# Six transfers of w_down for each expert, three of them between the next expert's first gate and up slices

## The reference, cut to what matters

```python
def expert_choice_ffn(h, w_router, w_gate, w_up, w_down):
    B, S, D = h.shape
    cap = EC_K * S // N_EXPERTS
    aff = jax.nn.softmax((h @ w_router).astype(jnp.float32), axis=-1)
    g, idx = lax.top_k(aff.transpose(0, 2, 1), cap)
    ...
    def run_expert(args):
        wg, wu, wd, ie, ge = args
        xe = h[b_rows, ie]
        he = jax.nn.silu(xe @ wg) * (xe @ wu)
        return (he @ wd) * ge[..., None].astype(h.dtype)
    ye = lax.map(run_expert, (w_gate, w_up, w_down, idx, g))
    return jnp.zeros_like(h).at[b_idx, idx].add(ye)
```

## Time and profile before

| What | Value |
|---|---|
| Median of three runs | 2459.91 us |
| The profiled execution's own time | 2462.03 us |
| Its span, from the first instruction to the last | 2460.2 us |
| TensorE busy | 1929.5 us (78%) |
| VectorE busy | 486.9 us (20%) |
| ScalarE busy | 315.1 us (13%) |
| Mean granted TensorE clock | 0.861 of full speed |
| Read from HBM | 688.96 MB |
| Chain that ended last | TensorE 49%, DMA 33%, SP's queue 8% |

### The profile page before, as it was taken

One profiled execution on the slowest core, in us unless ns is written; L12 is line 12 of the kernel. 1 busy time (PEld: TensorE's weight loads), 2 busy tenths in 40 slices (PEclk: granted clock), 3 DMA queues, 4 the chain that ended last, 5 costly groups with the idle time before them and its releaser, 6 DMA issues.

```text
span 2460.2 us, 28858 instructions
## 1 busy us (share of the span) xinstructions
PE 1929.5 (78%) x11352; PEld 1035.5 (42%) x11352; DVE 486.9 (20%) x1107; ACT 315.1 (13%) x733; POOL 41.2 (2%) x45
## 2 busy tenths in 40 slices
PE   8898999998999998987765666666666656766665
PEld 7774887588568855644211111111112211211111
DVE  3424332126333312152101010001001100110011
ACT  1213111022222100131100000000000000000001
POOL 0010000001010000000000000000000000000000
PEclk9999999999999999998887887787767777787777
DMA  7531543441245333326999999999999999999997
GB/s 257 138 65 39 184 154 120 157 161 64 69 129 180 129 145 128 137 79 275 407 392 422 421 417 419 422 421 418 418 423 421 419 417 424 420 418 418 424 421 315
DMA packets 173982, 694.24 MB, mean 282 GB/s; under 512 B 15452, under 2 KB 65436, under 8 KB 141010
## 3 DMA queue, kind: packets, MB, share of 16 engines
q1 hardware_dynamic: 170930, 683.63, 70.0%
q0 software_dynamic: 2832, 9.45, 1.9%
q10 hardware_dynamic: 144, 0.13, 0.0%
HBM read 688.96 MB, written 4.19 MB: 282 GB/s over the span
## 4 chain that ended last, share of the span: by engine, by line
PE 49%; DMA 33%; SPq 8%; DVE 4%; issue 3%; ACT 1%; DVEq 1%; ACTq 0%; POOL 0%; POOLq 0%
DMA arena<-in_w_up 29%; PE bank L543 20%; PE bank L564 9%; PE bank L954 5%; SPq L393 4%; DMA arena<-in_w_down 4%; SPq L389 3%; PE bank L969 2%; PE bank L550 2%; PE bank L683 1%; DVE arena L1596 1%; PE bank L692 1%; PE bank L753 1%; PE bank L601 1%; PE bank L767 0%
## 5 line engine op out<-in xcount | busy, mean ns | idle before, releaser
L954 PE MATMUL bank<-arena 128*32 128x512 f32 (+1 forms) x3072 | 482.2, 782 | 305.5 <-DMA arena<-in_w_up 264.2
L543 PE MATMUL bank<-arena 128*128 128x256 f32 (+1 forms) x2720 | 499.9, 345 | 6.8 <-ACT arena L991 3.4
L543 PEld LDWEIGHTS bank<-arena 128*128 128x128 f32 x2720 | 443.5, 192 | 62.8 <-issue 4.7
L954 PEld LDWEIGHTS bank<-arena 128*32 128x32 f32 x3072 | 111.6, 139 | 672.8 <-DMA arena<-in_w_up 358.0
L969 PE MATMUL bank<-arena 128*32 128x256 f32 x2816 | 255.3, 480 | 85.6 <-DMA arena<-in_w_down 85.5
L564 PE MATMUL bank<-arena 128*128 128x512 f32 x544 | 235.5, 593 | 1.2 <-ACT arena L1174 1.2
L969 PEld LDWEIGHTS bank<-arena 128*32 128x32 f32 x2816 | 84.5, 126 | 249.3 <-issue 218.3
L1596 DVE TENSOR_TENSOR arena<-arena,bank 64x256 f32<-64x256 f32 x96 | 38.6, 402 | 750.4 <-ACT arena L1193 748.7
L564 PEld LDWEIGHTS bank<-arena 128*128 128x128 f32 x544 | 102.7, 190 | 127.6 <-issue 126.1
L1193 ACT ACTIVATE arena<-bank 64x512 f32<-64x512 f32 (+1 forms) x48 | 23.2, 550 | 835.8 <-PE bank L954 835.8
L1475 DVE SCALAR_TENSOR_TENSOR arena<-bank,arena 128x254 f32<-128x254 f32 (+1 forms) x176 | 76.8, 478 | 194.6 <-ACT arena L1133 191.3
(11 more groups left out here) (259 smaller groups left out, 1205.1 us busy)
## 6 DMA issues: line engine op xcount, KB each, us to landing
arena<-in_w_down SPq DMA_DIRECT2D x364, 512.0 KB, 12.8
arena<-in_w_gate SPq DMA_DIRECT2D x128, 1408.0 KB, 19.4
arena<-in_w_up SPq DMA_DIRECT2D x128, 1408.0 KB, 22.4
arena<-in_w_up SPq DMA_DIRECT2D x44, 1024.0 KB, 7.5
arena<-in_w_in SPq DMA_DIRECT2D x40, 1024.0 KB, 7.4
arena<-in_w_down SPq DMA_DIRECT2D x16, 1024.0 KB, 5.6
arena<-in_w_out SPq DMA_DIRECT2D x12, 1024.0 KB, 7.1
bias_rows<-arena POOLq DMA_DIRECT2D x1, 3072.0 KB, 46.4
```

What stands on the lines that cost most here:

```text
L543: last = mm(ps[bank][:, j * S + lo:j * S + lo + n], w[:, k, c:c + P], xT[:, k, lo:lo + n], start=(k == 0), stop=(k == KT - 1))
L954: last = mm(ps[b][32 * q:32 * q + 32, 0:n], expert_x[:, k, :], gate_up_ring[:, s_, q // 2, c:c + n], start=(k == 0), stop=(k == KT - 1))
```

## The change

In the expert stage w_down is loaded in six pieces in place of 22 blocks. A half of w_down (1408 rows) is cut into pieces of 512, 512 and 384 rows (`PIECES`). In a piece of n rows each of the 128 partitions holds n/128 neighbouring rows of w_down, that is 4, 4 or 3 rows of 4 KB that lie one behind the other in memory. So a transfer is 2048 KB or 1536 KB, with 16 KB or 12 KB for each partition, and the ring is three buffers of 4, 4 and 3 rows, the same 11 rows as before. The multiplication that makes the hidden values (L1596) reads its inputs with a stride, so that the hidden rows come out in the order that the pieces have. TensorE's matmuls are the same in number and shape; it waits once for each piece and frees a buffer once for each piece.

SP's order changes too. For each expert it is now: slices 4 to 7, pieces 0, 1, 2, the next expert's slices 0 and 1, piece 3, the next expert's slice 2, piece 4, its slice 3, piece 5.

The diff, cut to its core:

```diff
-        down_ring = down_region.take(D_RING, D)
+        down_ring = [down_region.take(n // P, D) for _, n in PIECES]
...
-            def down(e, k):
-                sp.dma_start(down_ring[:, k % D_RING, :], a["w_down_2"][0, bass.ds(e, 1), k * P:(k + 1) * P, :].rearrange("o p n -> (o p) n")
-                             ).then_inc(sem(f"d_in{k % D_RING}"), 16)
+            def down(e, j, ahead=0):
+                b = j % len(PIECES)
+                c0, n = PIECES[b]
+                lo = j // len(PIECES) * HALF + c0
+                sp.dma_start(down_ring[b].rearrange("p r n -> p (r n)"), a["w_down_2"][0, ahead:][bass.ds(e, 1), lo:lo + n, :].rearrange("o (p r) n -> (o p) (r n)", p=P)
+                             ).then_inc(sem(f"d_in{b}"), 16)
...
-            stream_gate_up(0, range(GU_RING, KT))
-            stream_gate_up(1, range(0, 2))
-            stream_down(0, range(D_RING, FT))
-            stream_gate_up(1, range(2, KT))
-            stream_down(1, range(FT))
-            with sp.Fori(2, NE) as e:
-                stream_gate_up(e, range(KT))
-                stream_down(e, range(FT))
+            def expert_weights(e, ahead, first=False, last=False):
+
+                stream_gate_up(e, ahead, range(GU_RING, KT))
+                if not first:
+                    stream_down(e, ahead, range(3))
+                if not last:
+                    stream_gate_up(e, ahead + 1, range(0, 2))
+                stream_down(e, ahead, (3,))
+                if not last:
+                    stream_gate_up(e, ahead + 1, (2,))
+                stream_down(e, ahead, (4,))
+                if not last:
+                    stream_gate_up(e, ahead + 1, (3,))
+                stream_down(e, ahead, (5,))
+
+            expert_weights(0, 0, first=True)
+            with sp.Fori(0, NE - 2) as e:
+                expert_weights(e, 1)
+            expert_weights(0, NE - 1, last=True)
...
-                for k in range(FT):
-                    pe.wait_ge(sem("expert_hidden_copied"), e * 3 + (k // 4 + 1 if k < HT else 3))
-                    pe.wait_ge(sem(f"d_in{k % D_RING}"), e * (FT // D_RING * 16) + 16 * (k // D_RING + 1))
-                    for q in range(4):
-                        last = mm(ps[5][32 * q:32 * q + 32, 0:256], hidden_t[:, k % HT, 32 * (k // HT):32 * (k // HT) + 32], down_ring[:, k % D_RING, 256 * q:256 * q + 256],
-                                  start=(k == 0), stop=(k == FT - 1))
+                for j in range(CHUNKS):
+                    half, b = j // len(PIECES), j % len(PIECES)
+                    R = PIECES[b][1] // P
+                    if half == 0:
+                        pe.wait_ge(sem("expert_hidden_copied"), e * 3 + b + 1)
+                    pe.wait_ge(sem(f"d_in{b}"), e * 32 + 16 * (half + 1))
+                    for r in range(R):
+                        for q in range(4):
+                            last = mm(ps[5][32 * q:32 * q + 32, 0:256], hidden_t[:, 4 * b + r, 32 * half:32 * half + 32], down_ring[b][:, r, 256 * q:256 * q + 256],
+                                      start=(j == 0 and r == 0), stop=(j == CHUNKS - 1 and r == R - 1))
                     last.then_inc(sem("down_free"), 1)
...
-                        blocks = lambda y: y.rearrange("p (m n) -> p m n", n=P)[:, odd::2, :][:, 0:m, :]
+                        blocks = lambda y: y.rearrange("p (c r) -> p r c", c=P)[:, odd::2, :]
```

More of the change, by code:

```diff
@@ L44 @@
 UNITS_IN_2 = [0, 512, 1024, 1536, 2048, 2560]
-GU_RING, D_RING = 4, 11
+GU_RING = 4
 HALF = FF // 2
@@ L48 @@
 PIECES = [(0, 512), (512, 512), (1024, 384)]
+CHUNKS = 2 * len(PIECES)
 IN_BANKS = (0, 1, 4, 5, 0, 1, 6, 7, 4, 5)
@@ L384, in _, with gate_up @@
             sp.sem_inc(sem("gate_up_free"), GU_RING)
-            sp.sem_inc(sem("down_free"), D_RING)
-            def gate_up(e, k):
+            sp.sem_inc(sem("down_free"), len(PIECES))
+            def gate_up(e, k, ahead=0):
                 for n, w in enumerate(("w_gate_2", "w_up_2")):
-                    sp.dma_start(gate_up_ring[:, k % GU_RING, n, :], a[w][0, bass.ds(e, 1), k * P:(k + 1) * P, :].rearrange("o p n -> (o p) n")
+                    sp.dma_start(gate_up_ring[:, k % GU_RING, n, :], a[w][0, ahead:][bass.ds(e, 1), k * P:(k + 1) * P, :].rearrange("o p n -> (o p) n")
                                  ).then_inc(sem(f"gu_in{k % GU_RING}"), 16)
-            def down(e, k):
-                sp.dma_start(down_ring[:, k % D_RING, :], a["w_down_2"][0, bass.ds(e, 1), k * P:(k + 1) * P, :].rearrange("o p n -> (o p) n")
-                             ).then_inc(sem(f"d_in{k % D_RING}"), 16)
+            def down(e, j, ahead=0):
[4 more added lines that the diff above has]
+                             ).then_inc(sem(f"d_in{b}"), 16)
             sp.wait_ge(sem("projected_2"), 12)
@@ L401, in _ @@
             gate_up(0, 3)
-            for k in range(D_RING):
-                down(0, k)
+            for j in range(len(PIECES)):
+                down(0, j)
             sp.wait_ge(sem("rows_used"), (DEPTH + 1) * ROW_UNITS + 2)
@@ L406, in _, with stream_gate_up, stream_down @@
             gate_up(0, 2)
-            def stream_gate_up(e, ks):
+            def stream_gate_up(e, ahead, ks):
                 for k in ks:
[L410 to L416, removed]
-            stream_gate_up(0, range(GU_RING, KT))
-            stream_gate_up(1, range(0, 2))
-            stream_down(0, range(D_RING, FT))
-            stream_gate_up(1, range(2, KT))
-            stream_down(1, range(FT))
-            with sp.Fori(2, NE) as e:
-                stream_gate_up(e, range(KT))
-                stream_down(e, range(FT))
+                    sp.wait_ge(sem("gate_up_free"), e * KT + ahead * KT + k + 1)
+                    gate_up(e, k, ahead)
+            def stream_down(e, ahead, js):
+                for j in js:
+                    sp.wait_ge(sem("down_free"), e * CHUNKS + ahead * CHUNKS + j + 1)
+                    down(e, j, ahead)
+            def expert_weights(e, ahead, first=False, last=False):
[15 more added lines that the diff above has]
+            expert_weights(0, NE - 1, last=True)
             for t in range(T):
@@ L1197, in _ @@
                     last.then_inc(sem("expert_hidden_copied"), 1)
-                act.wait_ge(sem("down_free"), e * FT + FT + D_RING)
+                act.wait_ge(sem("down_free"), e * CHUNKS + CHUNKS + len(PIECES))
                 for q in range(2):
@@ L1594, in expert @@
                         m = 2 if odd == 0 or b < 2 else 1
-                        blocks = lambda y: y.rearrange("p (m n) -> p m n", n=P)[:, odd::2, :][:, 0:m, :]
+                        blocks = lambda y: y.rearrange("p (c r) -> p r c", c=P)[:, odd::2, :]
                         last = w.tensor_mul(hidden[64 * odd:64 * odd + 64, 2 * b:2 * b + m, :], blocks(expert_gate[0:64, c0:c0 + n]), blocks(ps[b][64:P, 0:n]))
                     last.then_inc(sem("expert_hidden"), 1)
-                v.wait_ge(sem("down_free"), e * FT + FT + D_RING)
+                v.wait_ge(sem("down_free"), e * CHUNKS + CHUNKS + len(PIECES))
                 for q in (2, 3):
```

## The result

The changed kernel takes 2710.65 us, the median of four runs (2708.92 to 2714.82), where the kernel before, now over four runs, takes 2460.78 (2458.36 to 2466.70). The ratio is 1.101, 95% interval 1.099 to 1.104. The prediction said 2730, from 2660 to 2768. The profiled execution took 2710.58 us with a span of 2708.8, against 2462.03 and 2460.2.

The account below looks back on a forecast made before the run. The prediction took transfers to bound the expert stage. Fourteen passages of 19.3 us gap less 1.0 faster w_down (256), 13.2 at the first and 0.8 at the last expert gave +270: 2730 us, range 2660 to 2768.

Parts of the forecast that it names:

- The bound: Expert stage: bound by its transfers and nothing else, 34.6 MB an expert at 420 GB/s, 82.4 us.
- Step 1, the larger transfers: w_down in rows of 12 or 16 KB: 425 GB/s in place of 410, gain 1.0 us an expert, 16 in all.
- Step 2, matmuls and hidden rows at nothing: Ahead of piece 3's issue: longer waits and the strided read lose nothing; a few us an expert without cover.
- Step 3, the gap: Behind piece 5 at each of 15 passages: no transfers for 19.3 us; 15.1 at full clock, 20.8 at the slowest rows.
- Passage 0: Between experts 0 and 1: gap of 19.3 less 6.1 already there, 13.2 us; faster w_down and late piece 3 about nil.
- The last expert: At the last expert: w_down 1.0 us faster, two more rows 1.8 us slower, in all +0.8 us.
- A: The forecast: gap behind piece 5 with TensorE mostly at half clock, 2730 us, 2700 to 2760; chance 0.66.
- B: Rival: same gap behind piece 5 with TensorE at full clock, 15.1 us each, 2666 us, up to 2700; chance 0.22.
- C: Rival: transfers not served in issue order, piece 5 lands early, out stage hidden, 2444 us; chance 0.04.
- D: Rival: over 2768 us, as 16 KB rows flow worse or piece 5's issue is held up, opening a second gap; chance 0.05.
- E: Rival: slice 4 issued early for an unseen reason, no change to measure, 2460 us; chance 0.03.
- a dry queue in a second place: Sign of a wrong prediction: the transfer queue also runs dry somewhere other than behind piece 5; no size given.

Follow-up runs that it names:

- behind3: Changed kernel with the next expert's slice 0 ahead of piece 3, slices 1 to 3 behind piece 5 (first expert: only 2 and 3 behind): 2446.38 us, ratio 0.993.
- ahead4: Changed kernel with all four of the next expert's slices ahead of piece 3, so pieces 3, 4 and 5 come in a row: 2676.37 us (one run).
- runs4k: behind3 with the same transfer sizes, but each partition's rows 512 KB apart, giving 4 KB runs, and the multiply without a stride: 2462.10 us, ratio 1.0007.
- behind4: Changed kernel with all four of the next expert's slices behind piece 5 (first expert: only 2 and 3 behind): 2470.78 us, ratio 1.003.
- behind1: Changed kernel with the next expert's slice 3 issued behind piece 5, slices 0 and 1 ahead of piece 3, slice 2 ahead of piece 4: 2574.49 us (one run).
- warm7: Changed kernel with seven added float32 matmuls of 512 columns behind piece 4, into a bank nobody reads: 2679.36 us (one run).
- warm: Changed kernel with four added float32 matmuls of 512 columns behind each of pieces 3 and 4, into a bank nobody reads: 2716.87 us, ratio 1.103.

## Why the prediction was right, point by point

Right in the number and in the mechanism: the loss is a stretch without transfers behind piece 5 at each passage, made up of the forecast's terms. The stretch came out 1.6 us shorter than forecast. The errors at the first and the last expert partly cancel; they are 5 us at most, so the number does not rest on luck. One statement did not hold: the queue does run dry in a second place.

**The bound.** Right. Period times flow is the expert's bytes in every kernel whose queue stays full: 82.4 us at 420 GB/s, 81.2 at 426 to 427.

**Step 1, the larger transfers.** Gain 1.0 us an expert by the forecast, 82.42 - 81.16 = 1.3 by behind3. The forecast took the 11 KB rows' 425 GB/s; the pieces flow at 428, by ahead4's rows and by the period: 81.16 less 8 x 6.78 us for the slices leaves 26.9 us for 11.53 MB. The 430 GB/s that the expectations of behind3 and runs4k give for the pieces was read from the window with gate and up slices. The mechanism was named as rows of 12 or 16 KB, and runs4k shows that it is these. The table of the Trainium skill's page DMA: Bandwidth & Descriptors (Bandwidth) that the prediction weighed was taken on transfers issued from GpSimd. It does not carry over to SP's queue here: transfers of 512 KB in 4 KB runs and of 2 MB in 4 KB runs flow at 410 and 412.

**Step 2, matmuls and hidden rows at nothing.** Right for experts 1 to 14. It had an edge that I saw only in part: the cover of piece 3's issue is pieces 0 to 2 and the two slices ahead of it. behind4 shows that without the slices it does not suffice. In the changed kernel itself it fails twice: at the first expert, where pieces 0 to 2 had landed long before, and at the last, which has no next slices.

**Step 3, the gap.** Its terms, as forecast and as the passage at 1432 has them: landing 1.8 and 1.5; from piece 5's first matmul to slice 0 12.4 (1.8 for the two rows and 10.6) and 12.1; slice 0 to the issue of slice 4 3.5 and 2.8; issue to bytes 1.6 and 1.3. Together 19.3 and 17.7. The largest miss is slice 0's. I had put it between the two clocks; the row of 9.65 us for 96 records is at full clock, for the clock has risen by the end of the placing. The other two latencies are 0.3 shorter than those I could read from windows of 5 us. The profiled execution came in 21 us under the forecast of 2732. These 1.6 us and 0.2 of flow are some 25 us over 14 passages. The last expert came out 2.7 under its forecast as well; the passage between the first two experts was 4.1 over it, and the stage started 1.4 later.

**Passage 0.** 13.2 forecast, 17.3 measured, the term that was off most for its size. Three windows there, piece 3's issue (at 1203.24), the last bytes, and the first bytes behind the gap:

```profile
1200.00:1205.00 5.00, 5.00 (x74) 2.49 (x76) 0.00 (x0) 0.39 (x1) 0.00 (x0) 0.77 0.49 160
1230.00:1235.00 5.00, 0.92 (x12) 0.46 (x16) 0.00 (x0) 0.00 (x0) 0.00 (x0) 0.50 0.41 175
1250.00:1255.00 5.00, 5.00 (x56) 1.58 (x52) 0.00 (x0) 0.00 (x0) 0.00 (x0) 1.00 0.55 191
```

At 427 GB/s bytes end at 1230 + 5 x 175/427 = 1232.05 and come again at 1255 - 5 x 191/427 = 1252.8. That is 20.7 us, with a placing and a slice 0 slower than at the later passage, and 6.1 of before are to be taken off: 14.6. The rest is piece 3, which waits for all of piece 0 and was issued into an empty queue: the first window has bytes for 1.9 of its 5 us. I had seen this as "some 1 us too late" and set it against the faster rows.

**The last expert.** 0.8 us longer by the forecast, 1.9 shorter as measured. The last bytes come at 2690 + 5 x 246/427 = 2692.9 (a window from 2690 to 2695 has 246 GB/s), 15.9 us ahead of the span's end, where before had 2460.2 - 2442.9 = 17.3. The placing took 3.70 us there against 5.40 before. Up to the last byte 0.5 is gained: w_down flows 1.2 us faster, and the window from 2675 to 2680, at piece 3's issue, has 332 GB/s, which is 1.1 us without bytes. The 1.8 us for two more rows at half clock did not come, as pieces 4 and 5 follow one another and the clock rises in them.

**The clock.** A against B was the main doubt, and the answer is A, but only in part: the granted clock is 0.50 at piece 5 and full again before slice 0. behind1, ahead4 and warm7, with full clock at the placing, give 15.2 to 15.6 us in the mean, and 14.7 where slice 0 is at full clock too, for B's 15.1. So the half clock is some 3 us of the 17.7. The Trainium skill, TensorE: Matmul & The Clock Gate, Part 1, says that activity releases the throttled clock. The traces agree: the pieces come with pauses of 6.81 and 8.49 us, the clock is 0.50 at piece 5, and in warm7, where it is 0.50 at piece 4, it is 1.00 from the added work on.

**C, D, E.** C is refuted by the window with 0 GB/s, and by the cover, which counts in order and one for one: with 0, 1, 2 and 3 slices behind piece 5 the period is 98.9, 89.7, 83.2 and 81.2. D would have needed under 373 GB/s, and pieces flow at 428. A second place where the queue runs dry exists, though at piece 3 and not, as in D, at piece 5: in behind4 at nearly every expert, in the changed kernel at the first expert (some 3 us) and the last (1.1 us). The prediction named a dry queue in a second place as a sign of being wrong. On that point it was wrong, by some 4 of 250 us. E has no trace: slice 4 was issued at 1448.31, after slice 0's matmuls.

## What to carry to other kernels

Before reordering a queue, find the last transfer that a serial stage waits for, and add up the latency from its last byte to the next issue that stage allows (here 15 to 18 us, behind3 being safe with 20): that much, in transfers already queued, must stand behind it, and each missing microsecond is paid in full. Ask the same at every place where a buffer is freed late, as larger pieces free it later. If prefetches are to go ahead of it, the consumer has to use them in that order too.

## What the runs showed of the hardware that was not expected

Run length in memory, not transfer size, set the flow: 428 GB/s for pieces with runs of 16 KB, 425 for gate and up with 11 KB, 412 for the same pieces with 4 KB runs and 410 for 512 KB blocks of 4 KB runs, at shares of 1.00 to 1.03. The runs do not show why.

TensorE's full clock was lost to a short pause. In warm it was 1.00 at the end of 4.2 us of added matmuls and through 3.24 us of idleness, and 0.50 from 2027 on, half a us into piece 5; piece 5 and the placing took 2.39 and 5.63 us, near the 2.79 and 5.67 of the kernel without the added work. In warm7, with 6.4 us of added matmuls and 0.51 us of idleness, it stayed at 1.00 and they took 1.50 and 3.70. The two kernels differ in the length of the work as well as in the pause, and the runs do not separate the two.
